# A hybrid decoder layer: the sources of all chunk states made together on four row groups, and three engine orders rewritten

## What is computed

```python
h += concat[ rwkv7(z), moba(q, k, v) ] @ w_mix_out       # z, q, k, v = rms_norm(h) @ w_in
h += cross_attention(rms_norm(h), rms_norm(mem))         # 4 heads
h += square(relu(rms_norm(h) @ w_ff1)) @ w_ff2
out = rms_norm(h)
# inside rwkv7, per token:
sa = einsum('bhvk,bhk->bhv', S, -kk_t)
S  = S * w_t[:, :, None, :] + sa[..., None] * (kk_t * a_t)[:, :, None, :] + v_t[..., None] * k_t[:, :, None, :]
y  = einsum('bhvk,bhk->bhv', S, r_t)
```

## Time and the profile before

| | |
|---|---|
| median of 3 runs | 486.78 us (486.06 to 487.11) |
| the profiled execution, its own time | 487.27 us |
| its span, first to last instruction | 485.5 us |
| PE busy | 463.2 us, 95% |
| DVE busy | 321.8 us, 66% |
| ACT busy | 237.1 us, 49% |
| mean granted TensorE clock | 0.996 |

### The profile page before, as it was taken

One profiled execution on the slowest core, in us unless ns is written; L12 is line 12 of the kernel. 1 busy time (PEld: TensorE's weight loads), 2 busy tenths in 40 slices (PEclk: granted clock), 3 DMA queues, 4 the chain that ended last, 5 costly groups with the idle time before them and its releaser, 6 DMA issues.

```text
span 485.5 us, 11051 instructions
## 1 busy us (share of the span) xinstructions
PE 463.2 (95%) x4774; PEld 433.1 (89%) x4774; DVE 321.8 (66%) x463; ACT 237.1 (49%) x359; POOL 34.0 (7%) x50
## 2 busy tenths in 40 slices
PE   3999999999789999999999998999999999999995
PEld 2989999998778989999998898999998989898983
DVE  3659688979856657777865488754646465555646
ACT  5667755443326225346445454563644454543534
POOL 8000000000000000034100045000000000000000
PEclk9999999999999999999999999999999999999998
DMA  7954654442230211455434055555555655655602
GB/s 249 299 170 133 217 171 132 141 165 90 90 91 26 89 50 53 162 174 174 140 121 160 14 175 175 174 173 174 174 189 193 207 190 175 218 185 202 204 15 86
DMA packets 61412, 73.10 MB, mean 151 GB/s; under 512 B 1314, under 2 KB 51572, under 8 KB 61364
## 3 DMA queue, kind: packets, MB, share of 16 engines
q1 hardware_dynamic: 61284, 72.14, 46.1%
q0 software_dynamic: 80, 0.26, 0.2%
HBM read 71.35 MB, written 1.05 MB: 149 GB/s over the span
## 4 chain that ended last, share of the span: by engine, by line
PE 81%; DVE 12%; issue 3%; ACT 2%; SPq 1%; DMA 1%; DVEq 0%; ACTq 0%
PE bank L475 14%; PE bank L477 13%; PE bank L476 13%; PE bank L492 6%; PE bank L493 6%; PE bank L494 6%; DVE w_lo L1520 3%; PE bank L442 2%; PE bank L443 2%; PE bank L444 2%; DVE op_lo L1583 2%; PE bank L840 1%; PE bank L864 1%; PE bank L604 1%; PE bank L754 1%
## 5 line engine op out<-in xcount | busy, mean ns | idle before, releaser
L1520 DVE TENSOR_TENSOR w_lo<-raw,w_hi 128x1024 fp32r<-128x1024 f32 x130 | 159.7, 1235 | 71.3 <-ACT w_hi L1029 71.0
L475 PE MATMUL bank<-op_hi,w_hi 128*128 128x256 f32 x672 | 193.6, 288 | 3.0 <-DVE w_lo L1520 2.3
L1029 ACT ACTIVATE w_hi<-raw 128x1024 fp32r<-128x1024 f32 x130 | 136.8, 1056 | 114.6 <-PE bank L477 64.3
L476 PE MATMUL bank<-op_lo,w_hi 128*128 128x256 f32 x672 | 190.0, 283 | 0.0
L477 PE MATMUL bank<-op_hi,w_lo 128*128 128x256 f32 x672 | 190.0, 283 | 0.0
L475 PEld LDWEIGHTS bank<-op_hi,w_hi 128*128 128x128 f32 x672 | 128.6, 191 | 6.3 <-issue 4.0
L476 PEld LDWEIGHTS bank<-op_lo,w_hi 128*128 128x128 f32 x672 | 128.8, 192 | 0.4
L477 PEld LDWEIGHTS bank<-op_hi,w_lo 128*128 128x128 f32 x672 | 128.7, 192 | 0.0
L492 PE MATMUL bank<-w_hi,op_hi 128*128 128x512 f32 x128 | 50.1, 391 | 0.0
L493 PE MATMUL bank<-w_lo,op_hi 128*128 128x512 f32 x128 | 49.9, 390 | 0.0
L494 PE MATMUL bank<-w_hi,op_lo 128*128 128x512 f32 x128 | 49.8, 389 | 0.0
(11 more groups left out here) (243 smaller groups left out, 511.5 us busy)
## 6 DMA issues: line engine op xcount, KB each, us to landing
raw<-in_w_ff SPq DMA_DIRECT2D x32, 1024.0 KB, 5.4
raw<-in_w_in SPq DMA_DIRECT2D x12, 1024.0 KB, 5.6
raw<-in_w_xkv SPq DMA_DIRECT2D x8, 1024.0 KB, 5.4
raw<-in_w_mix_out SPq DMA_DIRECT2D x4, 1024.0 KB, 5.4
raw<-in_w_xq SPq DMA_DIRECT2D x4, 1024.0 KB, 5.2
raw<-in_w_xo SPq DMA_DIRECT2D x4, 1024.0 KB, 5.1
xval<-in_x SPq DMA_DIRECT2D x2, 512.0 KB, 4.9
raw<-in_w_in SPq DMA_DIRECT2D x2, 512.0 KB, 5.8
```

The source lines that it names most:

```text
L475: mm(dst, wh[:, k, :], op_hi[which][:, k, :], start=first, stop=False)
L476: mm(dst, wh[:, k, :], op_lo[which][:, k, :], start=False, stop=False)
L1029: op(view(w_hi), r, ACT.Copy).then_inc(hi_done, 1)
L1520: tt(view(w_lo), r, view(w_hi).bitcast(f32), ALU.subtract).then_inc(lo_done, 1)
```

## The change

1. **Sources together.** `psi(n, p)` on PE now makes, for one pair of heads and for four chunks (three for n = 1), first the 8 (6) `btok` products, then the 8 (6) `ktok` products. The four chunks lie on the four groups of 32 rows, and chunk c goes to bank c mod 4. ACT copies the four banks to `s3` and `s4` (`source_out`), where they stay. The number of products is the same, 112.
2. **Decay in the transition.** `decay()` on DVE writes diagonal matrices of `pend` (two operations on 768 elements of each partition, with a 64 by 64 identity `eye` made in `sides`), and `phi(b)` on DVE adds them while it brings `PHI` out of PSUM: six operations on 256 elements on DVE in place of six copies on ACT. `state(c)` on DVE is then one addition, where there were three operations.
3. **Orders.** The lists of PE, ACT and DVE are rewritten. `mats` stands behind 38 quarters where it stood behind 55, `load(1, ...)`, `stats(1)`, `keys`, `tokens` and `bonus` move forward with it, and the quarters that came before are spread between `mats` and `states_out`. `copies(0)` comes before the second `load` on DVE, `params(1)` on PE two quarters later; `rms(3)` on ACT and `residual` on PE and ACT go into the last third.

```diff
+        sources = [flat(s3[:, :, :])[:, 0:512], flat(s3[:, :, :])[:, 512:1024], flat(s4[:, :, :])[:, 0:512], flat(s4[:, :, :])[:, 512:1024]]
...
+        def source(c):
+            return sources[c % 4][:, 256 * (c // 4):256 * (c // 4) + 256]
...
-            def psi(c):
-
-                if c == 0:
-                    pe.wait_ge(dve_q, 4)
-                elif c == 1:
-                    pe.wait_ge(act_phi, 1)
-                else:
-                    pe.wait_ge(dve_psi, c - 1)
-                r = slice(CH * (c % 4), CH * (c % 4) + CH)
-                for h in range(NH):
-                    dst = B[3 - c % 2][rows(h), 64 * (h // 2):64 * (h // 2) + 64]
-                    mm(dst, btok[r, c // 4, cols(h)], U[r, NH * (c // 4) + h, 0:HD], start=True, stop=False)
-                    last = mm(dst, ktok[r, c // 4, cols(h)], vtok[r, c // 4, cols(h)], start=False, stop=True)
-                last.then_inc(pe_psi, 1)
+            def place(c, h):
+
+                o = 256 * (c // 4) + 64 * (h // 2)
+                return B[c % 4][rows(h), o:o + 64]
+
+            def psi(n, p):
+
+                if n == 0 and p == 0:
+                    pe.wait_ge(dve_phi, 3)
+                tiles = [(c, h) for c in range(4 * n, min(4 * n + 4, NCH - 1)) for h in (2 * p, 2 * p + 1)]
+                for c, h in tiles:
+                    r = chunk(c % 4)
+                    mm(place(c, h), btok[r, n, cols(h)], U[r, NH * n + h, 0:HD], start=True, stop=False)
+                for c, h in tiles:
+                    r = chunk(c % 4)
+                    last = mm(place(c, h), ktok[r, n, cols(h)], vtok[r, n, cols(h)], start=False, stop=True)
+                if n == 1 and p == NP - 1:
+                    last.then_inc(pe_psi, 1)
...
+            def source_out(b):
+
+                act.wait_ge(pe_psi, 1)
+                n = 512 if b < 3 else 256
+                op(sources[b][:, 0:n], B[b][:, 0:n], ACT.Copy).then_inc(act_source, 1)
...
+            def decay():
+
+                dve.wait_ge(dve_side, 1)
+                dve.wait_ge(pe_mats, 2)
+                for i, x in enumerate((s3, s4)):
+                    last = tt(x[:, 0:3, :].rearrange("p c (h k) -> p c h k", h=NP),
+                              eye[:, :].unsqueeze(1).unsqueeze(1).to_broadcast([128, 3, NP, HD]),
+                              pend[:, :, 3 * i + 1:3 * i + 4].rearrange("p h c -> p c h").unsqueeze(3).to_broadcast([128, 3, NP, HD]),
+                              ALU.mult)
+                last.then_inc(dve_decay, 1)
+
+            def phi(b):
+
+                dve.wait_ge(pe_phi, 2)
+                dve.wait_ge(dve_decay, 1)
+                for i, x in enumerate((s3, s4)):
+                    last = tt(PHI[:, 3 * i + b, :, :].rearrange("p h k -> p (h k)"), B[b][:, 256 * i:256 * i + 256], x[:, b, :],
+                              ALU.add)
+                last.then_inc(dve_phi, 1)
 
             def state(c):
-                dve.wait_ge(dve_psi, c + 1)
+
+                dve.wait_ge(act_source, c % 4 + 1)
                 dve.wait_ge(pe_state, c)
-                tt(states[:, c, :, :], from_bank(c % 2), s4[:, :, 0:HD], ALU.add).then_inc(dve_state, 1)
+                tt(states(c), B[c % 2][:, 0:256], source(c), ALU.add).then_inc(dve_state, 1)
...
             key_sums()
-            dense(6)
+            dense(2)
             keys(0)
-            dense(19)
-            spread(1)
-            dense(1)
+            dense(2)
             load(1, 0)
             load(1, 1)
+            dense(12)
+            tokens()
             dense(2)
```

More of the change, by code:

```diff
@@ L962, in _ @@
             center()
-            pair_flip(3)
+            pair_scores(3)
             dense(2)
@@ L1438, in _ @@
             hi(88)
+            rms(3)
+            residual(0)
             hi(89)
+            follow(37)
+            take(38)
+            follow(38)
             take(39)
@@ L1452, in _ @@
             take(41)
+            follow(41)
             hi(98)
             hi(99)
-            follow(41)
+            residual(1)
             take(42)
@@ L1463, in _ @@
             hi(105)
+            residual(2)
+            residual(3)
             take(43)
@@ L1926, in _ @@
             load(0, 0)
+            copies(0)
             load(0, 1)
@@ L1982, in _ @@
             lo(22)
-            keys(3)
             lo(23)
+            mats(1)
+            blocks()
+            take(10)
             lo(24)
-            spread_copy(1)
-            sides()
-            take(10)
-            reads(1)
-            load(1, 0)
-            load(1, 1)
-            take(11)
-            lo(25)
-            reads(2)
-            lo(26)
-            tokens()
-            take(12)
-            lo(27)
+            lo(25)
             load(1, 2)
             load(1, 3)
-            lo(28)
@@ L2002, in _ @@
-            bonus()
-            lo(29)
-            bonus_bias()
-            mats(0)
-            take(13)
-            lo(30)
-            mats(1)
-            blocks()
-            take(14)
-            lo(31)
-            pair_scores(0)
-            inverse()
-            pair_weigh(0)
-            lo(32)
-            lo(33)
+            decay()
+            lo(26)
+            take(11)
+            lo(27)
+            inverse()
+            pair_scores(0)
+            lo(28)
             solve(2)
@@ L2018, in _ @@
             solve(3)
+            take(12)
+            pair_weigh(0)
             pair_values(0)
             pair_scores(1)
+            lo(29)
+            lo(30)
+            take(13)
+            pair_weigh(1)
+            lo(31)
+            outq(0)
+            outq(1)
+            lo(32)
+            take(14)
+            phi(0)
+            phi(1)
+            phi(2)
+            pair_values(1)
+            pair_scores(2)
+            pair_weigh(2)
             take(15)
-            pair_weigh(1)
+            lo(33)
@@ L2143, in _ @@
             lo(81)
-            follow(37)
+            follow(36)
+            rms(3)
             lo(82)
             lo(83)
-            follow(38)
             lo(84)
```

392 lines of the change are left out of this document (188 added, 204 removed).

## The result

The changed kernel takes 478.75 us in the median of 4 runs (478.35 to 479.23), the kernel before 486.60 us (486.06 to 487.11): a ratio of 0.984, 95% interval 0.982 to 0.986. The forecast was 478.1 us with a range of 474.5 to 483.5. The profiled execution took 479.23 us, with a span of 477.2 us and a mean granted clock of 0.994.

The account below looks back on a forecast made before the run. PE bounds the kernel, busy 463.2 of 485.5 us. From 487.27, terms -4.5, -1.2, -6.7, +4.0 and -0.3 give 478.6 profiled, so a median of 478.1 us, range 474.5 to 483.5.

Parts of the forecast that it names:

- sources: At the 224 source instructions on PE: spread over four row groups, 15.2 ns each instead of 35, gain 4.5 us.
- start: PE's start: quarter 0 begins near 10.5 us, clock rises earlier; gain 1.2 us, ends 0.3 and 1.5.
- stalls that go: PE's first 155 us: seven waits vanish, 5.5 us idle plus 1.2 us running empty, gain 6.7 us.
- stalls that come: Around mats and join, now earlier: PE waits for DVE, mainly 1.9 us at join; loss 4.0 us, ends nothing and 10.
- state chain: Between the six states: the way PE to DVE and back, 0.6 us, is hidden under one quarter; cost nothing.
- Rival B: At the sources: tiles of four row groups block each other, 35 ns stay; price 4.5 us, total 482.6; chance 0.12.
- Rival E: Across the new order: DVE keeps up, new stalls only 0.5 us; total 474.5 us; chance 0.08.
- F: Between states_out and first mix quarter: gains before 170 us lost again on ACT or DVE; 486 to 488 us; chance 0.02.
- DVE: Decay and phi on DVE: DVE gets 4.4 us of work and loses about 5.5 us; no PE time.
- C: First 105 us: DVE's queue too full, mats, blocks and join 5 to 6 us later; about 484 us; chance 0.17.
- D: Behind blocks: solve waits for inverse through DVE's 11.1 us backlog; 489 us if 11 us are lost; chance 0.03.
- Late places: Last xo units: a follow sits behind a lo; the 1.4 us stall shrinks by perhaps 0.3 us (0 to 0.7).

Follow-up runs that it names:

- experiment 12: Kernel after with old order at the last xo units, plus 20 single 8 by 8 products interrupting dense work in the last third: 481.60 us, ratio 0.989.
- experiment 6: Kernel after with the sources' products ordered chunk by chunk, neighbours on the same 32 rows and one bank: 487.62 us (1 run).
- experiment 7: Kernel after with each ktok product directly behind its btok product, on the same four row groups: 478.79 us (1 run).
- experiment 5: Kernel before with only the new sources and decay in the transition, orders otherwise old: 485.48 us, ratio 0.998.
- experiment 4: Kernel before with only params(1) on PE moved behind the first two quarters: 485.61 us, ratio 1.000.
- experiment 11: Kernel after with params(1) in front of the first two quarters again: 480.70 us, ratio 0.986 to the kernel before.
- experiment 8: Kernel after with the quarters between the six states moved in front of them: 482.32 us (1 run).
- experiment 2: Kernel after with only ACT's old order put back around the last xo units (hi(64), hi(67) behind their follow): 478.48 us (1 run).
- experiment 3: Kernel after with only DVE's old order put back around the last xo units: 476.95 us (1 run).
- experiment 10: Kernel of experiment 9 plus 20 identity transposes into an unused bank during the start: 475.32 us, ratio 0.975 to the kernel before.
- experiment 9: Kernel after with ACT's and DVE's old order put back around the last xo units: 475.83 us, ratio 0.976 to the kernel before.

## Why the prediction was right, and where it was off

| term | forecast | measured | from |
|---|---|---|---|
| sources | -4.5 | -4.9 | 224 instructions in 3.0 us, start to start |
| start | -1.2 | -2.7 | quarter 4 |
| stalls that go | -6.7 | -6.7 | all seven absent from the list of waits |
| stalls that come | +4.0 | +2.0 | `join` 1.1, issue gap 0.5, w_lo 0.4, start to start |
| state chain | 0 | 0 | states 2.24 us apart |
| xo units | -0.3 | +1.6, and +1.2 for the clock | quarters 132 to 136, and `rms(3)` |
| ten more interruptions | none | +2.0 | PE's starts in both kernels; 10 x 0.2 us by experiment 12 |
| sum | -8.7 | -7.5 | profiled executions: 487.27 to 479.23, -8.0 |

**Sources.** Right by mechanism and size: four row groups, and phi as the nearest row (15.2 ns against 13.4; the end of 10 ns was not reached). Experiment 6 shows that the row groups with their own banks do it, and experiment 7 that the order of the two products is worth little (0.2 to 0.7 us). Rival B falls. Rival E (0.5 us of new stalls) and F are not seen either. The estimate from the Trainium skill, page TensorEngine Tiling (Array Packing), section Performance Considerations, Instruction Overhead, would have been 25 ns for each; the trace shows about half of that. What the forecast missed is the price of rival B: it put 35 ns and 4.5 us there, but with the sources together on one row group the clock fell, and the kernel of experiment 6 takes 8.9 us more.

**The condition on the gain.** The forecast adds the sources' 4.5 us and the start as if they stood by themselves. They do not: alone, in the old orders, the sources gave 0.9 us of 4.9 (experiment 5) and the start 0.8 us of 1.25 (experiment 4) by the medians, neither told apart from nothing. In the new orders the start is worth 0.9 to 1.95 us (experiment 11, by ratios and by times). That the new orders are what lets the others through is the likely reading; the orders alone, without the new sources, were not run.

**State chain.** Cost nothing, as forecast; bare, a state shows 0.5 us (experiment 8), near the 0.6 the forecast named.

**DVE.** Its gain was counted too high: twelve operations of 0.42 us are 5.0 us and not "about 5.5". The two of `decay` took 0.95 us each, as estimated. Nothing in the sum rests on it.

**Start.** Mis-sized, 1.2 for 2.7. Quarter 0 came at 10.06 and not 10.5, and the clock's rise came earlier by more than the start did: 13.64 against just before 17.66. The step "if it rises as much earlier" was too careful, and its upper end of 1.5 us was passed. The rise is not fixed to the start: in the nine other profiles in which quarter 0 began between 9.6 and 10.7 it came between 11.4 and 14.5 us. So a part of this gain is the luck of the execution.

**Stalls that go.** Right in all seven places.

**Stalls that come.** `join` waited at 101.14 for 0.90 us, where the forecast had 1.9 us at 103.9: DVE was 2.8 us earlier than counted. The start, 1.5 us more than counted, is the likely source of half of that: in experiment 11, where PE is 2.2 us later, `join` is later too and waits the same 0.9 us. The rest is open. (The forecast's own sum is 93.4 + 10.3 = 103.7, so 0.2 us of it is a slip.) The w_lo wait at quarter 48 costs 0.4 us (forecast 0.7), at 104.37, and an issue gap at 84 us, which the forecast did not have, 0.5. Before keys, vtokens and pair_scores PE did not wait. Rivals C and D fall by this: `solve` never waits for `inverse`.

**Late places.** This is the term that failed. "One follow of the last xo units is behind a lo instead of beside GpSimd's squares; the 1.4 us stall loses perhaps 0.3 us". The stall grew from 1.4 to 3.0 us. The forecast followed what stands in front of `lo(68)` but did not ask whether the lo put forward, `lo(65)` and `lo(66)`, could start there: they wait for hi, and hi for ACT's part of `follow(30)` or for PE. It took DVE's order for the mechanism; experiments 2 and 3 show that the orders of ACT and DVE make it together. The clock that fell behind the stall, 1.2 us more, was in no term.

**Missing from the sum.** An interruption of the dense work costs about 0.2 us beside what stands in it, and the new order has ten more. The forecast took the work between quarters at its own price. Added up, the gain was underrated by 0.4 us in the sources, 1.5 at the start and 2.0 in the new stalls, and the cost by 3.1 us at the xo units and 2.0 for the interruptions: the errors cancel, and the total is better than its terms. That it came within 1 us is luck in this respect; the list of what is gained was right.

## What to carry to other kernels

When PE is freed in one stretch of an order written by hand, the gain may show only if the operands of the next stretch come earlier too (experiment 5), and each piece of other work put between dense matmuls has a price of its own (0.2 us here), so pieces that can stand together should. In a stretch bound by DVE, do not put an operation that has still to wait in front of one that is ready: write down what each item waits for, not its duration alone. Here that one place undone gives 475.83 us, 0.976 of the kernel before, and the idle products at the start 475.32 us, the best of all the versions.

## What the runs showed of the hardware

- The granted clock fell to 1.2 GHz for 3.41 us around the stall at the xo units in the kernel after (3.02 us idle) and in experiments 2 (3.04), 6, 7 and 8 (3.01 each), in experiment 4 behind 2.06 us idle with other gaps near it and again behind 1.47 us, and in experiment 8 also behind five gaps of 0.60 us, one in front of each state. It did not fall with 2.78 us idle (experiment 3), and not with 3.01 us in experiment 11. So these runs do not tell what decides it; where it fell at the xo units, it cost 1.0 to 1.2 us on top of the stall.
- From 150 to 160 us in experiment 6 PE was busy all the time and the granted clock was 0.50, while most of its products filled 32 rows of the array. The busy share alone does not show it.
- With 20 transposes of an identity in the first 8 us the clock rose at 6.72 us in place of 14.23 (experiments 10 and 9), and the first dense matmul began at 9.19.
- A single product of 8 by 8 between dense matmuls costs PE 0.3 us (experiment 12), with no idle time shown.
- One lo of 128x1024 took 1.91 us (usually 1.21) and two op_lo of 256 elements 2.67 us (0.87 with GpSimd idle) while GpSimd squared hT and added up the squares beside them (kernel after).
